# Two heads' attention value products issued as one pair, in alternation between the halves of their output bank

## What is computed

```python
def hybrid_layer(x, ...):                       # twice
    proj = h @ w_in                             # q, k, v, z of three branches, and `gates`
    ...
    s = jnp.einsum('bqhd,bkhd->bhqk', qi, k).astype(jnp.float32) * scale
    s = jnp.where(mask, s, NEG)
    p = jax.nn.softmax(s, axis=-1)
    o = jnp.einsum('bhqk,bkhd->bqhd', p.astype(v.dtype), v)
    ...
    branches = [y_a * silu(a_z), y_b * silu(b_z), y_c * silu(c_z)]
    proj_br = jnp.einsum('blnw,nwd->blnd', branches, w_branch)
    g = jax.nn.sigmoid(gates)                   # 3 x 1024 features
    return x + jnp.sum(g * proj_br, axis=2) @ w_out
```

## Time and profile before

| | |
|---|---|
| runs | 2714.74 us, median of 3 (2714.07 to 2715.06) |
| profiled execution, its own time | 2718.32 us |
| its span, from the first instruction to the last | 2716.5 us |
| PE busy | 2471.8 us (91%) |
| DVE, ACT, POOL busy | 1517.2, 1275.8, 877.0 us |
| mean granted clock of PE | 0.951 of full |

### The profile page before, as it was taken

One profiled execution on the slowest core, in us unless ns is written; L12 is line 12 of the kernel. 1 busy time (PEld: TensorE's weight loads), 2 busy tenths in 40 slices (PEclk: granted clock), 3 DMA queues, 4 the chain that ended last, 5 costly groups with the idle time before them and its releaser, 6 DMA issues.

```text
span 2716.5 us, 38856 instructions
## 1 busy us (share of the span) xinstructions
PE 2471.8 (91%) x15182; PEld 2068.0 (76%) x15182; DVE 1517.2 (56%) x2339; ACT 1275.8 (47%) x1850; POOL 877.0 (32%) x394
## 2 busy tenths in 40 slices
PE   7999989999978879868998879868999999999998
PEld 6877778877767868768997868767777777777775
DVE  2244461244454452682002452683998898899896
ACT  4534534524534343333222343323777677677674
POOL 4633355643344554445454554441000000000000
PEclk9999999999988989978999989977999999999999
DMA  5432234432252433224543433223999899899893
GB/s 160 142 107 78 94 109 121 138 111 79 94 120 93 125 110 109 94 94 139 186 163 101 126 110 109 94 93 133 378 354 344 334 355 347 332 351 352 331 352 139
DMA packets 255357, 489.16 MB, mean 180 GB/s; under 512 B 35096, under 2 KB 208696, under 8 KB 221128
## 3 DMA queue, kind: packets, MB, share of 16 engines
q1 hardware_dynamic: 227440, 483.74, 50.7%
q10 hardware_dynamic: 27080, 1.22, 0.7%
q0 software_dynamic: 656, 1.71, 0.2%
HBM read 485.57 MB, written 1.05 MB: 179 GB/s over the span
## 4 chain that ended last, share of the span: by engine, by line
PE 53%; DVE 11%; ACT 2%; issue 2%; POOL 1%; DMA 0%; DVEq 0%; SPq 0%; ACTq 0%
PE bank L676 18%; PE bank L1011 12%; PE bank L701 9%; PE bank L551 5%; PE bank L533 3%; DVE mem_high L2027 2%; DVE mem_high L2226 1%; PE bank L715 1%; PE bank L489 1%; PE bank L651 1%; PE bank L1052 1%; DVE mem_high L2183 1%; PE bank L466 1%; DVE mem_high L2203 1%; DVE mem_high L2024 1%
## 5 line engine op out<-in xcount | busy, mean ns | idle before, releaser
L1011 PE MATMUL bank<-memr 128*128 128x256 f32 (+5 forms) x8016 | 1091.8, 297 | 128.3 <-DVE mem_high L1963 23.9
L1011 PEld LDWEIGHTS bank<-memr 128*128 128x128 f32 (+3 forms) x8016 | 1034.2, 194 | 177.2 <-issue 42.0
L1377 POOL TENSOR_TENSOR memr<-mem_low,memr 128x1024 fp32r<-128x1024 f32 (+2 forms) x316 | 754.7, 2388 | 860.4 <-ACT memr L1454 849.4
L870 DVE TENSOR_TENSOR memr_tail<-mem_tail,memr_ring 128x2048 fp32r<-128x2048 f32 x198 | 451.8, 2289 | 59.7 <-ACT memr_ring L767 57.1
L676 PE MATMUL bank<-memr_ring,memr 128*104 128x512 f32 x1492 | 468.3, 399 | 3.8 <-DVE memr L875 3.8
L767 ACT CAST memr_ring<-mem_tail 128x2048 fp32r<-128x2048 f32 x198 | 379.2, 1916 | 129.4 <-PE bank L676 89.2
L1454 ACT CAST memr<-mem_low 128x1024 fp32r<-128x1024 f32 (+2 forms) x316 | 324.3, 1041 | 240.3 <-PE bank L1011 218.9
L676 PEld LDWEIGHTS bank<-memr_ring,memr 128*104 128x104 f32 x1492 | 251.1, 168 | 96.3 <-issue 4.0
L701 PE MATMUL bank<-memr_ring,memr 128*104 128x512 f32 x752 | 242.3, 400 | 1.7 <-DVE memr_ring L870 1.7
L676 PE MATMUL bank<-memr_tail,memr 128*104 128x512 f32 x536 | 211.9, 395 | 0.0
L701 PEld LDWEIGHTS bank<-memr_ring,memr 128*104 128x104 f32 x752 | 125.3, 168 | 42.9 <-DVE memr_ring L870 1.9
(11 more groups left out here) (241 smaller groups left out, 2605.7 us busy)
## 6 DMA issues: line engine op xcount, KB each, us to landing
mem_tail<-in_moe SPq DMA_DIRECT2D x198, 1024.0 KB, 4.9
mem_low<-in_w_in SPq DMA_DIRECT2D x112, 1024.0 KB, 5.1
mem_high<-in_moe SPq DMA_DIRECT2D x33, 1024.0 KB, 4.9
mem_low<-in_moe SPq DMA_DIRECT2D x33, 1024.0 KB, 4.9
mem_high<-in_ffn_w SPq DMA_DIRECT2D x30, 1024.0 KB, 8.5
mem_low<-in_w_branch SPq DMA_DIRECT2D x20, 1024.0 KB, 4.9
mem_low<-in_w_out SPq DMA_DIRECT2D x16, 1024.0 KB, 5.0
mem_low<-in_w_in SPq DMA_DIRECT2D x6, 512.0 KB, 3.9
```

The lines of the kernel that those rows point to most:

```text
L870: TTn(raw_r[n % RAW], raw[n % RAW], hi_f[n % HI], ALU.subtract).then_inc(family("m_split"), 1)
L1011: ins = pe.matmul(out(bank), lhsT, rhs, start=((k, i) == order[0]), stop=((k, i) == order[-1]))
L1377: pl(pool.tensor_tensor(low, raw, high, ALU.subtract), sig("w_split", i))
```

## The change

The value products of heads g and g+1 (g even) are issued together, as `pv_pair`. The matmuls alternate between the two heads, thus between the lower and the upper half of bank `OB`. PE issues the pair at the end of the even turn after them: turn i issues heads i-2 and i-1, and the odd turns have no value product. As the probabilities of an even head must now last one turn longer, there are four buffers of each kind; the new ones lie in `asc` and `tsc`.

```diff
+        late = asc.rearrange("p a b -> p (a b)")
+        ptm += [late[:, W2B * i:W2B * (i + 1)] for i in range(2)]
+        ptx += [late[:, 2 * W2B:2 * W2B + TA], tsc[:, 0, :]]
...
-        def pv(pe, g):
+        def pv_pair(pe, g):
 
             kind, hd = g % 24 // 8, g % 8
-            pe.wait_ge(*at("pt_act", g))
-            pe.wait_ge(*at("pt_dve", g))
-            if g % 2 == 0 and g >= 2:
+            for i in (g, g + 1):
+                pe.wait_ge(*at("pt_act", i))
+                pe.wait_ge(*at("pt_dve", i))
+            if g >= 2:
                 pe.wait_ge(*at("y_ready", g // 2 - 1))
-            v, v0 = ((vf, 64 * hd), (vm, 64 * hd), (vw, 64 * (hd // 4)))[kind]
-            o0 = 64 * (hd % 2)
-            for nk, t, rhs, q0 in ((META, 0, ptx[g % 2][0:META, :], 0), (P, 1, ptm[g % 2][:, 0:256], META),
-                                   (P, 2, ptm[g % 2][:, 256:384], META + P)):
-                ins = pe.matmul(OB[o0:o0 + 64, q0:TA], v[0:nk, t, v0:v0 + 64], rhs,
-                                start=(t == 0), stop=(t == 2), skip_group_check=True)
-            if hd % 2:
-                ins.then_inc(*sig("o_full", g // 2))
+            for t, nk, q0 in ((0, META, 0), (1, P, META), (2, P, META + P)):
+                for i in range(2):
+                    v, v0 = ((vf, 64 * (hd + i)), (vm, 64 * (hd + i)), (vw, 64 * (hd // 4)))[kind]
+                    rhs = (ptx[(g + i) % 4][0:META, :], ptm[(g + i) % 4][:, 0:256], ptm[(g + i) % 4][:, 256:384])[t]
+                    ins = pe.matmul(OB[64 * i:64 * i + 64, q0:TA], v[0:nk, t, v0:v0 + 64], rhs,
+                                    start=(t == 0), stop=(t == 2), skip_group_check=True)
+            ins.then_inc(*sig("o_full", g // 2))
...
                     feat3(("g", l, i), ch, i % 2 * P, P, TA)
-                    if i > 0:
-                        pv(pe, g - 1)
+                    if i > 0 and i % 2 == 0:
+                        pv_pair(pe, g - 2)
                 transposes(pe, 24 * l + 23)
-                pv(pe, 24 * l + 23)
+                pv_pair(pe, 24 * l + 22)
...
-                    st(cp(ptm[g % 2][:, :], TB[g % 2][:, 0:W2B]), sig("pt_act", g))
+                    st(cp(ptm[g % 4][:, :], TB[g % 2][:, 0:W2B]), sig("pt_act", g))
...
-                    st(V.tensor_copy(ptx[g % 2][0:META, :], XB[0:META, 0:TA]), sig("pt_dve", g))
+                    st(V.tensor_copy(ptx[g % 4][0:META, :], XB[0:META, 0:TA]), sig("pt_dve", g))
```

## The result

| | before | after |
|---|---|---|
| median | 2715.06 us (2714.07 to 2719.78, 7 runs) | 2731.83 us (2723.44 to 2734.19, 7 runs) |
| ratio to before | | 1.0048, 95% interval 1.0038 to 1.0057 |
| profiled execution, its own time | 2718.32 us | 2727.59 us |
| its span | 2716.5 us | 2725.8 us |
| mean granted clock of PE | 0.951 | 0.945 |

A forecast was written before the change was run, and what follows sets the result against it. PE was taken to bound the first block's attention loops. From 2718.3 us profiled, -10.0 (layers) -1.5 (old fall) +9.2 (falls) +0.5 (layer ends) gave 2716.5; lying 3.6 above the median, this became 2713.0 us, range 2704 to 2721.

The forecast's parts named there:

- The clock: First block's two attention loops: 22 waits cause 1 to 11 clock falls, taken as 6 of 1.53 us, 9.2 us.
- The third rival: PE's clock falls at most waits before the pairs (10 to 22): 2719 to 2737 us, slower; chance 0.16.
- rows 10: Second block's decay levels: clock full for 51.18 us around eight waits of about 1.1 us, cited for few falls.
- The wait: PE waits 0.87 us ahead of each pair for ACT's copy, late because POOL holds DVE's scaling.
- Two turns: An even and an odd turn of the attention loops take 11.93 us against 12.44, a gain of 0.5 us.
- the third kind: Heads of turns 16 to 23, with one more ACT operation before the exponentials: gain 0.3 us per two turns.
- A layer: Each layer's attention loop gains 5.0 us: 2.8 in turns 4 to 23 and 2.2 in the first turns.
- A longer fall at the end of a layer: After a layer's last gate product PE waits about 3.5 us instead of 2.1; 0.5 us added for a longer fall.
- fifth rival: The bank's halves don't run together: 24 pairs x 1.38 us more, 2737 us even without a fall; chance 0.03.
- The first turns: Turns 1 to 3 of a layer: pair starts at 213.57, turn 4 at 219.81 instead of 222.02, gaining 2.2 us.
- The fourth rival: DVE isn't held, as POOL's operation falls elsewhere: 16 us a layer gained, 2681 us; chance 0.05.
- The price of a fall: A clock fall to one half in the attention loops lengthens a turn from 6.22 to 7.75 us: 1.53 us.

The follow-up runs named there:

- the filled waits: Changed kernel with two products of constants (four matmuls) ahead of the waits for the copies in 11 pairs of each layer: 2712.02 us, ratio 0.9985.
- the run made for it: Changed kernel with the filling constant products ahead of one pair alone, that of turn 4 of layer 0: 2736.38 us, ratio 1.0065.
- the run with the shorter wait: Changed kernel with three waits ahead of the pair instead of five, ACT's copy of the later head last: 2721.83 us, ratio 1.0018.
- both (2682.1 and 2681.9): Changed kernel with the pair issued one turn later, 2682.05 us; changed kernel with ACT instead of DVE scaling the row maxima, 2681.93 us.

## Why the prediction failed

**The step that failed** is the count in "The clock": "1 to 11 falls. I take 6". The two loops have 16, over the upper bound too. That bound took one fall in two waits in the first turns as the odds of independent waits. They don't fall out as independent ones would: ten in a row in layer 0, none behind five pairs of layer 1 and then six in a row. That the falls are due to the idle time ahead of the pairs is shown by the filled waits. Why they come in series is not. A fall lengthens two turns from about 12.1 us to between 13.5 and 13.8, and the next fall comes 13.65 us after the last, so that the next pair stands at nearly the same place before it (2.2 to 2.6 us); that this is what carries a series on is an idea that the run made for it left open. In the changed kernel both series went on to the end of the loop; in the run with the shorter wait one ended after two falls, in the run with one filled wait one after six. The third rival had the count right (10 to 22). Its reason, "each fall shifts the next turns against the clock's own time, so that none is safe", fits the series but not the pairs that had none; with 0.16 it was given too little. The rule in "TensorE: Matmul & The Clock Gate" of the Trainium skill, section "A second HAM failure mode: psum-queue depth-cycling", was weighed there at the same low price. The trace of after agrees with it at 16 pairs of 22. Also, rows 10 were a poor witness: eight waits of that size with a full clock, but behind other work than this loop's.

**Terms of the sum that were mis-sized.**

- *The wait:* 0.87 forecast, 1.02 measured (a difference of 0.15). The pair starts 0.21 us after the end of ACT's copy (644.45) and in the kernel before 0.06 after it (207.68 + 0.45 to 208.19). Part of this is the waits queued behind ACT's: with only the later head's, and ACT's last, two turns were 0.07 shorter. The other 0.08 is not explained.
- *Two turns:* 11.93 forecast, 12.07 measured: a gain over 12.43 of 0.36 instead of 0.5. In the third kind it is 0.13 instead of 0.3 (12.30 us between two pairs without a fall in the execution with one filled wait).
- *A layer:* 6 x 0.36 + 4 x 0.13 - 1.40 + 2.2 = 3.5, both 7.0 instead of 10.0.
- *A longer fall at the end of a layer:* 0.5 us added, and not borne out. The falls at the last pairs lasted 3.41 us in both layers (before, 3.41 and 6.82).

With these, -7.0 - 1.5 + 16 x 1.53 = +16.0 us; the medians differ by 16.8. So close a match is partly luck, since the 16 falls are those of one execution. In the two profiled executions themselves the loops account for 15.4: the second loop starts 10.2 us later than before (617.27 against 607.11), and to its end (775.74 against 760.30) another 5.3 are lost. Behind them, where nothing was changed, after was 6.1 us quicker, which is why the profiled executions differ by 9.3 only:

```profile
760.30:2716.50 1956.20, 1762.55 (x10403) 1475.09 (x10402) 1216.78 (x1469) 940.58 (x1076) 522.07 (x225) 0.94 0.58 207
...
775.74:2725.80 1950.06, 1755.79 (x10404) 1469.80 (x10402) 1217.41 (x1469) 940.39 (x1076) 522.85 (x225) 0.94 0.58 207
```

The first row is before, the second after. The same matmuls took PE 6.8 us less, so the 6.1 us are the clock's too: its records add up to 231 us at half clock behind the loops before, and to 216 us after. No run shows that the change has a part in that. The profiled execution of before lay 3.3 above its median, that of after 4.2 below.

**What held.** The pair costs 1.41 us (1.42); the halves run side by side (fifth rival refuted), but in this pair only because it alternates, a condition that I hadn't separated. The first turns came out to the hundredth (scores of turn 4 at 219.81, the pair at 213.59 against 213.57), and that is luck: the scores of turn 2 came 0.24 us earlier than forecast (207.08 against 207.32), and the wait behind them was as much longer (1.27 us instead of 1.04; DVE's scaling took 2.15 us there). DVE is held in even turns at 1.99 us and not in odd ones; taking its operation away took the wait away. That it is POOL that holds it is read from the ends, which agree to 0.03 us whether the hold is 2.15, 1.99 or 1.17 us; no run took POOL's operation away. The fourth rival's sum for a kernel without that wait, 2681 us, was met by both (2682.1 and 2681.9), by other means. The price of a fall (about 1.5) and the free buffers were right. The last pair of layer 1 was expected to wait about 3.5 us; PE idles 3.42 there.

## What to carry to other kernels

If work is taken off the engine that is the bound, ask what the removed work had covered; here a 1.40 us product had covered a 1.99 us hold on another engine, and moving the pair one turn later changed a loss of 0.5% into a gain of 1.3%. Price a short idle gap in a tight TensorE loop not by its length (1.02 us) but with the clock: count the falls in the trace after, look whether they come in series, and treat gaps of a loop as one risk, not as many small ones. Float32 matmuls of 64 output columns for two halves of a bank can run side by side at half the cost, but the order in the program can decide it: alternate them, and measure.

## What I had not expected of the hardware

- Falls of the clock come in series: every 13.65 us, where two turns without a fall take 12.07 us; 78 us of the same loop passed without one.
- Four useless matmuls in each gap are cheaper than the gap: 2712.02 against 2731.83 us.
- Two heads' products for different halves, issued head by head, take 2.79 us, just as in one half; alternating 1.41. In the second block a head-by-head order of shorter products did overlap (eight matmuls in 1.03 us).
